# Scan of a hybrid backbone kernel: couplings issued a level earlier, and unit products added on TensorE

## What is computed

```python
h_lat = rmsnorm(x, norm1_g[l]) * (1.0 + sc1) + sh1
... = split_cols(h_lat @ w_in[l], IN_SIZES)       # Fourier, attention, recurrent mixing, gates
y_ctx, s_ctx = rwkv_mix(pr_c, zero_state, *rw)
y_lat, _ = rwkv_mix(pr_l, s_ctx, *rw)             # bidirectional, starts from the context's state
def step(S, inp):                                 # inside rwkv_mix, 8 heads of 64, two directions
    sa = jnp.einsum('bhvk,bhk->bhv', S, at)
    S = S * wt[:, :, None, :] + sa[..., None] * bt[:, :, None, :] + vt[..., None] * kt[:, :, None, :]
    return S, jnp.einsum('bhvk,bhk->bhv', S, rt)
...                                               # merge by sigmoid gates, then a top-2 mixture of experts
```

## Time and profile before

| | us |
|---|---|
| median of three runs | 2342.22 |
| the profiled execution | 2353.76 |
| its span, first to last instruction | 2352.0 |
| scan of layer 0, in the span | 426 to 612 |
| scan of layer 1, in the span | 1612 to 1821 |

### The profile page before, as it was taken

One profiled execution on the slowest core, in us unless ns is written; L12 is line 12 of the kernel. 1 busy time (PEld: TensorE's weight loads), 2 busy tenths in 40 slices (PEclk: granted clock), 3 DMA queues, 4 the chain that ended last, 5 costly groups with the idle time before them and its releaser, 6 DMA issues. The chain is left out here.

```text
span 2352.0 us, 49452 instructions
## 1 busy us (share of the span) xinstructions
PE 2112.7 (90%) x21626; PEld 1341.5 (57%) x21626; DVE 682.5 (29%) x1672; ACT 540.6 (23%) x1260; POOL 266.3 (11%) x461
## 2 busy tenths in 40 slices
PE   6999999799899999999999599998998999987784
PEld 2454444688544444445556465556997787744442
DVE  1033334766331011210010214455465311200001
ACT  2123322455320001201111223323354301110011
POOL 0000000444000001101111200002333000011111
PEclk8999989889999999999999799996579999999897
DMA  7148717000122122539999711110000345799993
GB/s 286 69 155 345 294 37 253 3 4 4 55 90 107 54 92 96 223 111 390 397 397 389 275 37 51 61 50 2 3 3 8 151 149 190 271 382 400 393 403 118
DMA packets 55811, 399.64 MB, mean 170 GB/s; under 512 B 6672, under 2 KB 22928, under 8 KB 33648
## 3 DMA queue, kind: packets, MB, share of 16 engines
q1 hardware_dynamic: 43440, 361.94, 40.1%
q0 software_dynamic: 8576, 23.08, 2.6%
q10 hardware_dynamic: 3648, 12.45, 1.7%
HBM read 365.47 MB, written 31.98 MB: 169 GB/s over the span
## 5 line engine op out<-in xcount | busy, mean ns | idle before, releaser
L535 PE MATMUL ps<-H,memory 128*128 128x512 f32 (+2 forms) x1728 | 615.9, 513 | 8.8 <-DMA memory<-in_w_in 7.0
L535 PEld LDWEIGHTS ps<-H,memory 128*128 128x128 f32 (+1 forms) x1728 | 328.3, 191 | 284.9 <-issue 251.5
L1080 PE MATMUL ps<-memory 128*32 128x256 f32 x5120 | 302.1, 398 | 46.6 <-DMA memory<-in_eu 45.1
L535 PE MATMUL ps<-memory 128*128 128x512 f32 (+3 forms) x928 | 320.3, 496 | 6.7 <-issue 3.0
L1080 PEld LDWEIGHTS ps<-memory 128*32 128x32 f32 x5120 | 179.8, 115 | 164.9 <-issue 71.1
L535 PEld LDWEIGHTS ps<-memory 128*128 128x128 f32 (+1 forms) x928 | 173.9, 188 | 144.9 <-issue 127.5
L889 PE MATMUL ps<-memory 64*64 64x32 f32 x5120 | 223.1, 244 | 17.9 <-POOL memory L2042 6.9
L889 PEld LDWEIGHTS ps<-memory 64*64 64x64 f32 x5120 | 209.4, 164 | 28.5 <-POOL memory L2042 10.2
L1105 PE MATMUL ps<-memory 128*32 128x256 f32 x2560 | 144.8, 380 | 4.9 <-ACT memory L1468 3.8
L2042 POOL TENSOR_TENSOR memory<-memory,cons 128x256 f32<-128x256 f32 x160 | 113.2, 728 | 100.4 <-DVE memory L1725 78.8
L1105 PEld LDWEIGHTS ps<-memory 128*32 128x32 f32 x2560 | 80.0, 110 | 59.5 <-ACT memory L1468 10.1
(11 more groups left out here) (268 smaller groups left out, 2019.0 us busy)
## 6 DMA issues: line engine op xcount, KB each, us to landing
memory<-in_eg SPq DMA_DIRECT2D x32, 2048.0 KB, 16.6
memory<-in_eu SPq DMA_DIRECT2D x32, 2048.0 KB, 21.9
memory<-in_ed SPq DMA_DIRECT2D x32, 2048.0 KB, 22.8
memory<-in_w_ada SPq DMA_DIRECT2D x24, 2048.0 KB, 9.4
memory<-in_w_in SPq DMA_DIRECT2D x20, 2048.0 KB, 7.4
expert_rows<-memory SPq DMA_DIRECT2D x4, 3456.0 KB, 23.7
memory<-in_w_out SPq DMA_DIRECT2D x4, 2048.0 KB, 8.2
memory<-expert_rows ACTq DMA_DIRECT2D x19, 384.0 KB, 10.3
```

The costliest lines, as they stand in the source:

```text
L535: ins = mm(ps[0:M, bank, 0:w], lhs(k), rhs(k), start=(k == 0), stop=(k == n - 1))
L1080: ins = mm(out_.rearrange("p (x n) -> p x n", x=2), XGT[:, k, g * GROUP:g * GROUP + GROUP], sets[b][:, 0:2, k * 512 + c * P:k * 512 + c * ...
```

## The change

A helper `fill(n, w)` issues n products of the unit matrix with the first w columns of `H`, into the last w columns of PSUM bank 0; nothing reads them. It stands at these places: 11 products 512 wide between the last projection and the handover ahead of the scan; 128 wide ones ahead of level 1 (5 in step 0, 2 in steps whose predecessor had no readout), ahead of level 3 (6 in step 0, 2 in every other step) and ahead of level 4 (6 in step 0, 2 in steps whose predecessor had no readout); and 3 products 512 wide behind the last readout. In layer 0 only step 0 counts as one without a predecessor's readout; in layer 1 these are steps 0 to 4.

`couple(0)` now stands ahead of the first `grams`, and `couple(k + 1)` stands at level 4 of step k, between the joins and the grows. It no longer waits for the last level of the inverse, but for the first one.

```diff
+                def fill(n, w):
+                    for _ in range(n):
+                        mm(ps[:, 0, 512 - w:512], ident, H[:, 0, 0:w], start=True, stop=True)
...
                 for u in range(6, 2 * RJ):
                     lora_up(u)
+                pe.wait_ge(sem("rin_copied"), RT * l + RT)
+                fill(11, 512)
                 handover("pe", pe)
...
                         pe.wait_ge(sem("keys"), nth(N, d))
                         if N:
-                            pe.wait_ge(sem("inverse"), inverses(N - 1, 5, d))
+                            pe.wait_ge(sem("inverse"), halved(N - 1, 1, d))
...
+                couple(0)
                 for k in range(STEPS):
                     grams(k, 0)
                     if k:
                         values(k - 1)
-                    couple(k)
                     grams(k, 1)
+                    spare = not k or not streams(l, k - 1)
                     for n in range(len(LEVELS)):
+                        if n == 1 and spare:
+                            pe.wait_ge(sem("masked"), nth(l * STEPS + k, 0))
+                            fill(2 if k else 5, P)
+                        if n == 3:
+                            if k + 1 < STEPS:
+                                pe.wait_ge(sem("turned"), carried(l, k, 0))
+                            fill(2 if k else 6, P)
+                        if n == 4 and spare:
+                            fill(2 if k else 6, P)
                         join(k, n, 0)
...
                         join(k, n, 1)
                         if k and n == 0:
                             correct_values(k - 1)
+                        if n == 4 and k + 1 < STEPS:
+                            couple(k + 1)
                         grow(k, n, 0)
                         grow(k, n, 1)
...
                 readout(STEPS - 1)
+                fill(3, 512)
                 handover("pe", pe)
```

## The result

| | before | after |
|---|---|---|
| median of seven runs, us | 2339.11 | 2316.06 |
| the runs, us | 2331.74 to 2348.1 | 2311.03 to 2319.52 |
| profiled execution, us | 2353.76 | 2315.11 |
| its mean granted clock | 0.92 | 0.953 |
| median over the timed runs of the mean granted clock | 0.929 | 0.954 |

The change is faster: 0.9892 of the time before, with a 95% interval of 0.9867 to 0.9918. That is 23 us where 54 were forecast; the time lies inside the range, 28 us above the forecast.

What follows compares the result with a forecast made beforehand. Low clock was taken as the first matter. Terms summed to -68.5 us from 2353.76, 2285.3; one dip per scan made 2294.1, half of the profiled run's 11.5 us excess off gave 2288; range 2262 to 2325.

Steps and rivals of the forecast that it cites:

- item 3: Scan starts: the first coupling fills TensorE's wait for queries; -2.9 us in layer 0, -2.0 in layer 1, together -4.9.
- one dip per scan: Allowance in both scans for the clock still falling: one dip of about 10 us each, +4.4 us each.
- items 4 to 6: Full clock saves 4.4 and 8.3 us (step 0), 10.1 (layer 0 dips), 30.6 and 4.5 (layer 1, steps 1-4).
- Items 4 and 8: Narrow fills in step 0 and in steps 1 to 7, half charged as hidden: +3.6 and +4.7 us.
- Item 7: Couplings ahead of level 4's grows: masks and first joins 1.0 us earlier in 14 steps, -14 us; nothing at half clock.
- Items 2, 4, 6 and 9: Wide products around the scans cost nothing; at full clock step 0 takes 16.3 us, layer 1's sparse steps 18.6.
- The profiled run: Profiled execution before is 11.5 us above the timed median, from profiling or low clock; half was taken off.
- The clock holds in part: Rival, layer 1 steps 0 to 4: half of their 43.4 us stays, 2310 us; chance 0.24.
- The narrow fills are paid: Rival, layer 1 steps 0 to 4: fills don't act on the clock; 2347 us, up to 2359; chance 0.11.
- point of decision: Fills are paid when low clock saved times 0.4 is under their 22 us: under 55 us saved, of some 190.
- accident of one run: Rival: layer 1's long half-clock stretch belongs to the profiled run only, 2321 us; chance 0.05.
- Starved grows: Rival at level 4: late keys hold the coupling and both grows, up to 1 us a step, +14 us.

Runs made afterwards that it cites:

- e1: The change with all fills left out, only the couplings moved; 2310.93 us, ratio 0.9882 to the kernel before.
- e7: The change without the narrow pairs ahead of level 3 in steps whose predecessor had a readout; ratio 0.9881 to the kernel before.
- e5: The kernel before with couplings moved and the 512 wide products, no narrow ones; ratio 0.9923.
- e6: The kernel before with couplings moved, the wide products and only step 0's 17 narrow ones; ratio 0.9893.
- e8: The kernel before with two narrow unit products ahead of the second grams of each step from step 1 on; ratio 1.0073.
- e13: The kernel before with three narrow unit products directly ahead of update in every step from 1 on; ratio 1.0079.
- e3: The kernel before with only the 11 and 3 wide unit products, couplings in the old place; 2350.43 us, ratio 1.0038.
- e10: The kernel before with couplings moved behind the grows of level 4, no unit products; ratio 0.998.
- e2: The kernel before with all fills of the change, couplings at their old place and wait; 2352.78 us, ratio 1.0043.
- e4: The kernel before with only the narrow unit products in the steps, couplings in the old place; 2357.77 us, ratio 1.0076.
- e9: The kernel before with a second, silent set of the next step's couplings at level 4, the old set kept; ratio 1.0059.
- e12: The kernel before with couplings moved directly behind update, ahead of level 4's second join, no unit products; ratio 0.9926.

## Why the forecast was right in direction and too large

**Where the difference lies.** The sum gave 59.7 us for the scans (2353.76 to 2294.1); they gained 27.6. Start of the scans: 4.9 us forecast (item 3), 3.3 + 1.9 measured. Low clock (items 4 to 6, less the one dip per scan): -4.4 - 8.3 - 10.1 - 30.6 - 4.5 + 8.8, -49.1 us; measured 122 us fewer at half clock, which is 49 us at 0.40 each and 41 at the fit's 0.34. Fills: +3.6 and +4.7 forecast, some 21 to 25 us paid. Couplings: -14 forecast, between nothing and 10 us gained, as below. So the fills cost 13 to 17 us more, the couplings gave 4 to 14 less, the clock up to 8 less; together they make up the 32 us, and the fills are the part that is sure. The forecast of 2288 also took 6 us off for the profiled execution, and outside the scans 11 us came off: 32 - 11 + 6, and 1 us by which the median of after lies above its profiled execution, are the 28 us by which the forecast was low.

**Items 4 and 8, the fills: the step that failed is "charged half".** A narrow product was priced at 0.21 us and half of it taken as hidden. The timeline of after, a pair ahead of level 3 at full clock:

```profile
493.30 0.71 PE L728 MATMUL ps<-H,cons 128*128 128x128 f32 x4
...
493.95 0.66 PE L896 MATMUL ps<-memory 64*64 64x32 f32 x16
```

The join behind the pair starts 0.65 us after the pair began, so 0.32 us each. The mean of the five full-clock steps is 21.07 us, 0.64 above e1's 20.43; against e7's four of the same steps, which have no pair either and lie between 20.45 and 21.18, the excess is only 0.28, so single steps scatter by as much as a pair costs. Over all full-clock steps behind one with a readout (the last step of each scan left out), the change's eight average 20.80 us, the 26 of e1, e5, e6 and e7 that have neither pair nor old couplings 20.21: 0.3 us a product. At half clock e8 and e13 give 0.53 to 0.58 each. In step 0 they were cheaper. First e5, without narrow products, then e7, with 17:

```profile
422.35:441.69 19.34, 16.88 (x402) 15.99 (x404) 14.58 (x38) 6.04 (x19) 11.21 (x17) 0.79 0.01 4
424.33:444.41 20.08, 18.67 (x439) 17.60 (x441) 14.37 (x39) 5.81 (x19) 11.07 (x17) 1.00 0.01 3
```

At 0.40 for its 8.1 us of half clock e5's step comes to 16.1 us, so the 17 products cost some 4 us, 0.23 each. That makes 34 x 0.23 + 44 x 0.3 to 78 x 0.32, 21 to 25 us in all, where the forecast had 8.3. TensorE works in order, and the waits for VectorE that were to cover the products hid little of them.

**Item 7, the couplings ahead: the step that failed is "the first joins follow by as much".** VectorE's wait for couplings did go. Its waits in the scan of layer 0 after, as total, times, longest:

```profile
DVE memory L1769 <- PE ps L896: 44.4, 30, 4.7
...
DVE memory L1745 <- PE ps L784: 0.7, 1, 0.7
```

and before:

```profile
DVE memory L1749 <- PE ps L889: 31.2, 28, 3.7
DVE memory L1725 <- PE ps L777: 17.0, 8, 4.0
```

and in e1, which has no fills (L1757 and L1762 are the additions of L1749 and L1754):

```profile
DVE memory L1757 <- PE ps L894: 34.7, 29, 2.1
...
DVE memory L1762 <- PE ps L894: 7.0, 12, 2.1
```

The 17.0 us on couplings, 4.0 of them at the start of the scan, became 0.7. But the wait at the additions rose from 31.2 to 44.4; the fills have a part in that, and without them it is 34.7, with 7.0 at the last level, where it was 4.0 (L1754). The timeline of after at the same place as the earlier trace rows shows why:

```profile
481.10 0.29 DVE L1774 TENSOR_TENSOR memory<-memory,ps 128x128 f32<-128x128 f32 x1 [0.17 <-PE ps L896]
...
481.30 0.42 DVE L1745 TENSOR_TENSOR memory<-ps,cons 128x256 f32<-128x256 f32 x1
...
482.30 0.44 PE L795 MATMUL ps<-cons,memory 64*128 64x64 f32 x8
...
482.77 1.19 ACT L1337 COPY memory<-ps 64x512 f32<-64x512 f32 x2 [0.90 <-PE ps L795]
...
484.10 0.95 PE L896 MATMUL ps<-memory 64*64 64x32 f32 x26 [0.42 <-ACT memory L1337]
```

The mask starts while the last addition ends. But the first join follows that addition by 2.7 us (481.39 to 484.10), where it was 3.0 (468.79 to 471.80): it now waits for ScalarE's copy of the transposed values, which stand behind the first `grams` on TensorE. That is 0.3 us won, and the coupling ahead of the grows delays the last addition by up to its 0.69 us. Only the mask's wait had been looked at, not what else the join needs.

What the move is worth by itself at full clock can be read from the steps at 1.00 behind one with a readout, without unit products, in all traces. With the couplings in the old place they average 20.81 us (before, five) and 21.05 (e3, six); ahead of the grows 20.36 (e1, seven), 19.99 (e5, six), 20.10 (e6, six) and 20.33 (e7, seven); behind the grows 21.02 (e10, six). So it is some 0.7 us a step, not 1.0, and only ahead of the grows. "Nothing at half clock" was off too: e10 has 28.45 us against the 28.79 of the earlier trace rows, 0.34 us a step. Over 14 steps that is 5 to 10 us; the account of the table, with nothing for it, and the fit, with about 4 us beyond the start, leave room for less. No run separates the couplings' own worth from the price of low clock.

**What carries the clock.** The prediction gave the saving of half clock to the unit products alone. Here it failed in mechanism: with the couplings moved and no fill, half clock goes from 186 to 101 us, the clock of the timed runs from 0.928 to 0.942 and the time to 0.9882. Fills alone raise the clock as much (e2, 0.940), but pay for it; on top of the couplings they take half clock to 64 us and, at their price, bring nothing more. That items 4 to 6 came out near right in sum is therefore luck in part: a second cause, not in the sum, did a share of the work.

**Items 2, 4, 6 and 9**: the wide products lie in idle time in the traces, as said (the first mask comes 10.3 us behind the last projection in the change, 10.7 in e1, which has none), and the scan begins at full clock. Why e3's runs are slower all the same is open. Layer 1's sparse steps were to take 18.6 us; e7's whole one at 1.00 takes 19.72, 1.1 more, which its six narrow products, 1.9 us at 0.32, more than make up. Step 0 was to take 16.3 us without fills, and e5 bears that out (16.1 above); in the change it takes 21.40 and 21.34, for its 17 narrow products and 3.4 us still at half clock. The half clock that was left is 64 us, where one dip a scan, some 20, was expected: most of it in steps 1 to 3 of layer 1 and in the tail of layer 0.

**The profiled run.** Half of the 11.5 us between it and the median was taken off. After the change the profiled execution is 0.95 us under the median, and that of before had some 40 us more half clock than its median run, at 0.34 to 0.40 each 14 to 16 us. So nothing speaks for a cost of profiling, and all of it should have come off.

**The rivals.** "The clock holds in part" said 2310 and was nearest; it named the right symptom, steps of layer 1 partly at half clock. "The narrow fills are paid" was right on the price (22 us of fills; 21 to 25 measured), wrong in that they don't act on the clock, and it missed that the couplings save clock. Its point of decision, some 52 to 62 us of half clock saved at 0.40, is not tested sharply: e2 saved 66 against the profiled execution of before and still lost 10 us in its timed runs, e4 saved 20 and lost 18. The stretch in layer 1 is no accident of one run: e3, e8, e10 and e13 show it too, though the profiled execution of before had more half clock than its median run. Starved grows: the wait at the last additions rose by 3 us in the scan of layer 0 (e1), far from a microsecond a step. In e10, three whole steps stayed at 0.50 with TensorE busy for 28.15 of 28.45 us, so the rule of the Trainium skill, "TensorE: Matmul & The Clock Gate", Part 1, that activity releases the throttle, does not hold here if activity is read as the profile's busy time. The same page of the Trainium skill, "HAM oscillation", prices low clock at half of its time; the scans here show 0.34 to 0.40.

**What stays open.** What about the coupling's place lifts the clock. Dense work by `update` alone does not (e13), a shorter head of the step alone does not (e10), and a silent coupling at the place, with the head as before, does not show in the timed runs (e9). Only the two together do: the coupling out of the head and ahead of the grows (e1, and in part e12, where it stands still earlier). Nor is it known whether the clock follows the order of the work or the time that the delayed grows and the earlier masks shift; no run holds one fixed.

## What to carry to other kernels

Test the parts of a change alone: here the part meant for the clock cost what it brought, and a reordering of real work, costed at a microsecond a step, raised the clock. Unit products on an engine that works in order and is 90% busy cost most of their time or all of it, so place them only where a wait is longer than they are. Before reading a change of clock from one profiled execution, hold it against the clock of the timed runs: in e9 the half clock of the profiled execution was lower than before's and the clock of the timed runs was not higher. When a wait is removed from one engine, look for what else the next consumer needs before booking the gain.

## What was unexpected in the hardware

The granted clock is decided by something finer than how busy TensorE is: products of 64 by 64 by 32 and 64 by 64 by 64 kept it at 0.50 for some 85 us with TensorE 99% busy (e10), while the same work, with the couplings ahead of the grows instead of behind them, ran at 0.92 (e1, steps 2 and 3). Half clock cost 0.34 to 0.40 us for each microsecond of it: with 0.40 the account of the table comes within 8 us in all fourteen kernels. And a 128 wide unit product, 0.21 us by its share of a 512 wide one, costs 0.32 us where a pair stands ahead of a join, 0.23 in step 0, where TensorE waits more, and 0.53 to 0.58 at half clock.
